# A two-block layer kernel on one core: the first loads and splits in another order, products of x's high parts one tile ahead of its low parts, key products in front of decay and rate products

## The reference

```
mod = silu(c) @ w_ada + b_ada                    # six rows of 1024: shift1, scale1, gate1, shift2, ...
h = rms_norm(x, norm1_w) * (1 + scale1) + shift1
proj = h @ w_in                                  # q, k, v (convolved), z, gates, ...
x = x + gate1 * (mix @ w_o)
h2 = rms_norm(x, norm2_w) * (1 + scale2) + shift2
x = x + gate2 * ((a_path * v_path) @ ffn_w_down) # a_path, v_path from h2 @ ffn_w_up
# second block
p = token_shift(rmsnorm(x, norm1_g_2) @ w_in_2, mu)
r, k, v, wd, ad, gd = split(p)
w = -softplus(-(w0 + tanh(wd) @ w_decay_up)) - 0.5    # decay
a = sigmoid(a0 + ad @ a_up)                           # rate
k = k * (1 + (a - 1) * k_a)
```

## Time and profile before

| what | value |
|---|---|
| median of 3 runs | 2097.0 us (2096.62 to 2098.36) |
| the profiled execution | 2096.3 us, span 2094.5 us |
| TensorE matmul busy | 2009.4 us, 96% of the span |
| VectorE, ScalarE, GpSimd busy | 898.6, 817.8, 989.5 us |
| DMA | 199.59 MB, mean 95 GB/s |
| chain that ended last | TensorE 87%, VectorE 5%, ScalarE 2%, issue 2%, DMA 2%, GpSimd 1% |

### The profile page before, as it was taken

The page is one execution under the profiler, slowest core; times in us unless marked ns, Lnnn a source line. Parts: engine busy times, 40 slices in busy tenths (PEclk is TensorE's granted clock), DMA queues, the critical chain, the costliest instruction groups (busy, mean ns, idle before and its releaser), DMA issues.

```text
span 2094.5 us, 26186 instructions
## 1 busy us (share of the span) xinstructions
PE 2009.4 (96%) x10110; PEld 1630.2 (78%) x10110; DVE 898.6 (43%) x1492; ACT 817.8 (39%) x1092; POOL 989.5 (47%) x767
## 2 busy tenths in 40 slices
PE   6999999999999999999999898999999999999997
PEld 3786896877778887888888577977987788888886
DVE  1678454777432224222200576347974531211101
ACT  3567224336563234232222553334326643222221
POOL 3647614655204564655655372004453265565662
PEclk9999999999999999999999897999999999999999
DMA  6311105631112322222223221003421222222222
GB/s 280 101 61 61 41 1 220 267 105 61 41 41 101 140 87 80 97 101 101 101 101 126 85 69 53 1 31 115 123 90 61 101 101 99 85 98 101 101 101 80
DMA packets 30827, 199.59 MB, mean 95 GB/s; under 512 B 5488, under 2 KB 7664, under 8 KB 9712
## 3 DMA queue, kind: packets, MB, share of 16 engines
q1 hardware_dynamic: 30704, 197.92, 26.2%
HBM read 188.99 MB, written 4.19 MB: 92 GB/s over the span
## 4 chain that ended last, share of the span: by engine, by line
PE 87%; DVE 5%; ACT 2%; issue 2%; DMA 2%; POOL 1%; SPq 0%; ACTq 0%; DVEq 0%; POOLq 0%
PE ps L444 24%; PE ps L445 23%; PE ps L446 23%; PE ps L504 2%; DMA ar<-ada_dram 1%; PE ps L871 1%; PE ps L534 1%; DVE ar L2039 1%; PE ps L858 1%; PE ps L638 1%; PE ps L966 1%; PE ps L926 1%; DMA raw<-panels_dram 1%; PE ps L1176 1%; POOL WL L2570 0%
## 5 line engine op out<-in xcount | busy, mean ns | idle before, releaser
L2570 POOL TENSOR_TENSOR WL<-raw,WH 128x512 fp32r<-128x512 f32 x588 | 780.2, 1327 | 885.6 <-ACT WH L1331 849.2
L444 PE MATMUL ps<-hH,WH 128*128 128x512 f32 x1648 | 660.5, 401 | 20.4 <-DVE xL L1928 6.1
L446 PE MATMUL ps<-hH,WL 128*128 128x512 f32 x1648 | 647.6, 393 | 0.0
L445 PE MATMUL ps<-arR,WH 128*128 128x512 f32 x1392 | 542.2, 390 | 0.0
L1331 ACT CAST WH<-raw 128x2048 fp32r<-128x2048 f32 x147 | 280.9, 1911 | 518.0 <-DMA raw<-panels_dram 516.9
L444 PEld LDWEIGHTS ps<-hH,WH 128*128 128x128 f32 x1648 | 313.5, 190 | 101.2 <-issue 33.9
L446 PEld LDWEIGHTS ps<-hH,WL 128*128 128x128 f32 x1648 | 313.1, 190 | 67.0
L445 PE MATMUL ps<-xL,WH 128*128 128x512 f32 x848 | 336.2, 396 | 0.0
L445 PEld LDWEIGHTS ps<-arR,WH 128*128 128x128 f32 x1392 | 261.7, 188 | 54.4 <-issue 0.2
L444 PE MATMUL ps<-arR,WH 128*128 128x512 f32 x592 | 230.6, 390 | 0.0
L446 PE MATMUL ps<-arR,WL 128*128 128x512 f32 x592 | 230.3, 389 | 0.0
(11 more groups left out here) (391 smaller groups left out, 2259.5 us busy)
## 6 DMA issues: line engine op xcount, KB each, us to landing
raw<-panels_dram SPq DMA_DIRECT2D x145, 1024.0 KB, 4.8
ar<-ada_dram SPq DMA_DIRECT2D x12, 2048.0 KB, 11.9
xT<-xT_dram SPq DMA_DIRECT2D x2, 2048.0 KB, 8.6
out_dram<-xT SPq DMA_DIRECT2D x8, 512.0 KB, 2.6
ar<-ar SPq DMA_DIRECT2D x12, 256.0 KB, 6.8
xT<-out_dram SPq DMA_DIRECT2D x1, 2048.0 KB, 9.2
wide<-wide_dram SPq DMA_DIRECT2D x1, 1024.0 KB, 6.9
ar<-ar SPq DMA_DIRECT2D x8, 128.0 KB, 4.0
```

Source lines behind the costliest of these rows:

```text
L444: mm(out, lhs[0], rhs[0], start=first, stop=False)
L445: mm(out, lhs[0], rhs[1], start=False, stop=False)
L446: return mm(out, lhs[1], rhs[0], start=False, stop=final)
L2570: ins = tt(WL[:, n % SLOTS, c], raw[:, n % SLOTS, c], WH[:, n % SLOTS, c].bitcast(F32), ALU.subtract)
```

## The change

1. SyncE issues block 2 between panel 0 and panel 1 instead of behind both.
2. `panel_due` is -1 for panel 0 and 0 for panel 1, so the two are split apart. ScalarE casts panel 0 ahead of `rstd` and panel 1 behind the copy of rows 2. GpSimd splits panel 0 and then waits for the fourth low part before panel 1.
3. TensorE does the column sums ahead of columns 0; rows 1 and columns 1, rows 3 and columns 3 stand together, behind the first halves of projections 0 and 1 and ahead of those of 2 and 3.
4. In `project_by_k` and `first_projections` the two products with the high part of tile k stand ahead of the product with the low part of tile k - 1, with a wait for each part of its own.
5. In the second block `rkv` 5 stands ahead of `wup` and `rkv` 6 ahead of `aup`; VectorE's `mix(2)` stands ahead of the scans.

The diff, without context lines (line numbers of before, then of the changed kernel):

```diff
@@ -238 +238 @@
-            return 0 if n < 2 else panel_part[0] if n == 2 else panel_part[n - SLOTS + 1]
+            return n - 1 if n < 2 else panel_part[0] if n == 2 else panel_part[n - SLOTS + 1]
@@ -459,0 +460,5 @@
+            def high_products(out, w, x, first):
+
+                mm(out, w[0], x[0], start=first, stop=False)
+                mm(out, w[1], x[0], start=False, stop=False)
+
@@ -464,0 +470,6 @@
+
+                def weights(j, k):
+
+                    c = slice((jobs[j][1] % per) * P, (jobs[j][1] % per + 1) * P)
+                    return [x[:, k, c] for x in ws[j]]
+
@@ -466,4 +477,9 @@
-                for k in range(kt):
-                    pe.wait_ge(*ready(k))
-                    for j, (stage, i) in enumerate(jobs):
-                        last_of[j] = product(pst(stage, i), [x[:, k, (i % per) * P:(i % per + 1) * P] for x in ws[j]], src(k), k == 0, k == kt - 1)
+                for k in range(kt + 1):
+                    if k < kt:
+                        pe.wait_ge(*ready("high", k))
+                        for j, (stage, i) in enumerate(jobs):
+                            high_products(pst(stage, i), weights(j, k), src(k), k == 0)
+                    if k:
+                        pe.wait_ge(*ready("low", k - 1))
+                        for j, (stage, i) in enumerate(jobs):
+                            last_of[j] = mm(pst(stage, i), weights(j, k - 1)[0], src(k - 1)[1], start=False, stop=(k == kt))
@@ -544 +560 @@
-                project_by_k([("up" + sfx, 0), ("up" + sfx, 1)], h_ff, lambda k: norm_step("low", norm, k))
+                project_by_k([("up" + sfx, 0), ("up" + sfx, 1)], h_ff, lambda part, k: norm_step(part, norm, k))
@@ -600,4 +616,10 @@
-                    for k in range(lo, hi):
-                        if j == 0:
-                            pe.wait_ge(*norm_step("low", "rms1", k))
-                        ins = product(pst("qkv", i), [x[:, k, (i % 2) * P:(i % 2 + 1) * P] for x in w], h_mix(k), k == 0, k == KD - 1)
+                    out, c = pst("qkv", i), slice((i % 2) * P, (i % 2 + 1) * P)
+                    for k in range(lo, hi + 1):
+                        if k < hi:
+                            if j == 0:
+                                pe.wait_ge(*norm_step("high", "rms1", k))
+                            high_products(out, [x[:, k, c] for x in w], h_mix(k), k == 0)
+                        if k > lo:
+                            if j == 0:
+                                pe.wait_ge(*norm_step("low", "rms1", k - 1))
+                            ins = mm(out, w[0][:, k - 1, c], h_mix(k - 1)[1], start=False, stop=(k == KD))
@@ -610,2 +631,0 @@
-                pe.wait_ge(sem("one_in_32"), 1)
-                ada_columns(0)
@@ -615,0 +636,2 @@
+                pe.wait_ge(sem("one_in_32"), 1)
+                ada_columns(0)
@@ -619 +640,0 @@
-                ada_rows(1)
@@ -620,0 +642 @@
+                ada_rows(1)
@@ -623 +644,0 @@
-                first_projections(2, 0, HALF)
@@ -624,0 +646 @@
+                first_projections(2, 0, HALF)
@@ -886 +908 @@
-                project_by_k([("wo", 0), ("wo", 1)], mixed, lambda k: part_ready("low", "mix", k))
+                project_by_k([("wo", 0), ("wo", 1)], mixed, lambda part, k: part_ready(part, "mix", k))
@@ -900 +922,2 @@
-                project_by_k([("wag", 0), ("rkv", 4)], h_mix, lambda k: norm_step("low", "rms3", k))
+                project_by_k([("wag", 0), ("rkv", 4)], h_mix, lambda part, k: norm_step(part, "rms3", k))
+                project("rkv", h_mix, 1, i0=5)
@@ -906 +929 @@
-                project("rkv", h_mix, 1, i0=5)
+                project("rkv", h_mix, 1, i0=6)
@@ -910 +933 @@
-                project("rkv", h_mix, 2, i0=6)
+                project("rkv", h_mix, 1, i0=7)
@@ -1191 +1214 @@
-                project_by_k([("wout", 0), ("wout", 1)], merged, lambda k: part_ready("low", "merged", k))
+                project_by_k([("wout", 0), ("wout", 1)], merged, lambda part, k: part_ready(part, "merged", k))
@@ -1236,2 +1259 @@
-            for n in range(2):
-                load_panel("qkv", QKV_ORDER[2 * n] // 2, n)
+            load_panel("qkv", QKV_ORDER[0] // 2, 0)
@@ -1238,0 +1261 @@
+            load_panel("qkv", QKV_ORDER[2] // 2, 1)
@@ -1467 +1490 @@
-                split(0)
+                split(-1)
@@ -1470,0 +1494 @@
+                split(0)
@@ -2329,0 +2354 @@
+                mix(2)
@@ -2334 +2358,0 @@
-                mix(2)
@@ -2602,0 +2627,2 @@
+                split(-1)
+                pool.wait_ge(*norm_step("low", "rms1", HALF - 1))
```

More of the change, by code:

```diff
@@ L618, in block_1 @@
                 first_projections(0, 0, HALF)
+                first_projections(1, 0, HALF)
                 ada_rows(1)
-                first_projections(1, 0, HALF)
                 ada_columns(1)
                 ada_rows(3)
+                ada_columns(3)
                 first_projections(2, 0, HALF)
-                ada_columns(3)
                 first_projections(3, 0, HALF)
```

## The result

| what | before | changed |
|---|---|---|
| median (runs) | 2097.7 us (4: 2096.6 to 2102.7) | 2079.4 us (4: 2073.1 to 2082.4) |
| the profiled execution | 2096.3 us, span 2094.5 | 2082.4 us, span 2080.6 |

The ratio is 0.9904, with a 95% interval of 0.9875 to 0.9933. The forecast was 2079.1. The four runs of the changed kernel lie between 2073.1 and 2082.4, so that the forecast meets the median to 0.3 us is luck.

A forecast was written before the change was run, and what follows sets the result against it. TensorE was taken as the bound, its matmuls busy 2009.4 of 2094.5 us. Savings of 5.5 + 1.7 + 2.2 + 7.8 = 17.2 us from 2096.3 gave 2079.1, range 2073 to 2086.5.

The forecast's parts named there:

- Start, 5.5: At the start, new loads, splits and order on TensorE save 5.5 us, between 3.8 and 6.1.
- GpSimd now waits ...: 0.95 gone: At the start, VectorE's first three scaled tiles no longer run beside GpSimd's split of panel 1; 0.95 us saved.
- The rows 2 block ... is no later than now: At the start, modulation block 2, issued ahead of panel 1, arrives no later than before; no gain counted.
- the break at 18.14 is just what is removed: At the start, unbroken TensorE work from 14.50 may raise the clock near 20, saving 2.3 us more.
- Ahead of the feed-forward, 1.7: First product starts once high part 0 is ready, 1.7 us earlier; ends 0 and 2.3.
- Rival (a): In VectorE-paced stretches and projections behind them the low clock stays, costing 41 us: 2127, slower than before; chance 0.02.
- Second block's first norm and key products, 2.2 + 7.8 = 10.0: Second block: earlier first product saves 2.2 us; key products ahead of the decay products remove stop and slow products, 7.8.
- fills idle time: Second block: mix 2 ahead of the scans uses time in which the scans wait 7.1 us for ScalarE's sigmoids.
- Rival (b): At line 926 TensorE stops for VectorE's key chain, keeping 3.6 of the 7.8 us: 2083.4; chance 0.13.
- (c): At the start, panel 1 lands late and holds ScalarE, first product at 36.7: 2086.8 in all; chance 0.04.
- (d): At the feed-forward and in the second block the low clock eats the earlier start: 13.3 us gained, 2083.0; chance 0.10.
- The gains travel to the end: Behind each changed place TensorE is the bound again and releases the next panels, so the whole 17.2 us lasts.

The follow-up runs named there:

- s_no_gpsimd_wait: Changed kernel without GpSimd's wait for the fourth low part, so it splits panel 1 as soon as it is cast; start stretch 72.9 us against 66.7.
- s_old_sums: Changed kernel with the column sums behind columns 0 again; start stretch 67.3 us against 66.7.
- only_byk: Kernel before with the new order of products in `project_by_k` only; median 2093.1 us, ratio 0.9978.
- best: Changed kernel with rows 3 ahead of columns 1 and modulation columns 10 behind key-value projection 7; median 2070.6 us, ratio to before 0.9871.
- k_mix_back: Changed kernel with VectorE's mix 2 behind the four scans again; one time, 2081.8 us.

## Why the prediction was right, and where it was not

- **The time.** 2079.1 forecast, 2079.4 measured. The range and most terms hold, but the closeness is luck: the start was forecast 2.3 too small, the loss of 2.8 in the middle was not forecast, the two about cancel, and the same kernel measured again had 2076.9.
- **Start, 5.5; measured 7.8.** The mechanism was mis-sized at one step and wrong at another. "GpSimd now waits ...: 0.95 gone" was taken from an execution in which only the first of the three scaled tiles lay beside the split; with VectorE's tiles earlier more lie beside it: in s_no_gpsimd_wait four of its first five operations take 1.65 each, and the clock stays low behind them. The wait is worth up to 6.2 in the changed kernel (5.5 without the later first tile). "The rows 2 block ... is no later than now" was costed at nothing; the load order is worth 2.3. The high products first, 1.6, measured 1.3. The step on the clock, "the break at 18.14 is just what is removed", is refuted by s_old_sums: with the break back, the sums took 2.82. The early clock did come in the changed kernel (sums and columns 0 take 3.79 together in place of 7.31), but not from where the prediction took it, and without the other pieces it is worth little: 0.4 at the first product in only_byk. What decides the moment stays open. Twice 0.8 lost was right, and best takes it back.
- **Ahead of the feed-forward, 1.7; measured 2.4.** In five of nine executions with the new order in this place the stretch is 366.0 to 366.9, in the other four 367.9 to 368.0, against 368.4 to 369.2 in the four without it: at the least 0.4. In the changed kernel the first product comes 0.1 us behind its high part, and the clock is 1.00 from 784 to 790, as its window shows:

```profile
784.00:790.00 6.00, 5.71 (x25) 4.61 (x26) 5.72 (x9) 3.33 (x6) 0.00 (x0) 1.00 0.01 3
```

- **Rival (a) and the rule behind it.** Products paced by VectorE, with short gaps, ran at the full rate in that window. They do not always: in the other four of the nine executions the first six microseconds of this stretch stand at 0.51 to 0.53. In s_old_sums, for one:

```profile
784.00:790.00 6.00, 5.80 (x14) 4.58 (x15) 5.72 (x9) 3.32 (x6) 0.00 (x0) 0.50 0.01 3
```

In all nine the next six are at 1.00. So the low level of rival (a) is real, but here it never outlasts the stretch, and the stretch is still 0.4 to 1.2 us shorter than in the four kernels of the old order. Its price of 41 us did not come. By the rule named in the prediction, of the Trainium skill ("TensorE: Matmul & The Clock Gate", section "A second HAM failure mode: psum-queue depth-cycling"), short idle moments between groups of products would have kept the clock moving between its levels here; the window of the changed kernel at 784 us, at 1.00, does not agree. In s_no_gpsimd_wait the gaps are longer, up to 1.3 us in its list of waits, and there the clock did stay low.
- **Second block's first norm and key products, 2.2 + 7.8 = 10.0; measured 10.4.** Alone, the new order of products gives 2.7 and the keys 9.0, so they overlap by 1.3. The stop is gone and the decay products take 3.70, as forecast. Right in the sum, but that mix 2 "fills idle time" is not why its move matters: k_mix_back shows that it hands a bank back in time.
- **Rival (b).** VectorE's last key operation ends at 1211.23, and TensorE comes at 1213.71: the cover shrank from 3.6 to 2.5 and held. The rival's sum, 17.2 less 4.2, gives 2083.3 and not 2083.4.
- **Rivals (c) and (d).** Panel 1 was cast 24.73 to 26.63 and held nothing back. (d) is in part what the four executions with the low clock at the feed-forward show: 0.4 to 1.2 us left of the 1.7 there.
- **"The gains travel to the end".** True behind 1230, within what executions differ by: the rest is 863.2 before, and 861.5 and 866.9 in two executions of the changed kernel. False in the middle, where "TensorE is the bound" does not hold at columns 10: TensorE came there early, stopped 5.8 us instead of 1.3, and met the low clock behind it. The stop there is 1.3 to 1.5 in the four kernels with the old start or only its GpSimd wait, and 3.4 to 6.8 in seven of the eight with the new start and the old place of columns 10 (middle 695.7 to 697.1 in them); the eighth, k_mix_back, has 1.7 and 692.7. "Waits of some us at places that are free now" was one of the prediction's own signs of being wrong, and this is one. The place before, TensorE and VectorE:

```profile
431.88 1.31 PE L590 MATMUL ps<-cm,ar 128*128 128x1 f32 x8 [1.32 <-DVE ar L2039]
422.30 9.52 DVE L2039 SCALAR_TENSOR_TENSOR ar<-ar,st 128x512 f32<-128x512 f32 x7
```

and VectorE's in k_mix_back:

```profile
414.25 8.61 DVE L2063 SCALAR_TENSOR_TENSOR ar<-ar,st 128x512 f32<-128x512 f32 x7
```

Coming early is only one part. These seven operations take 11.28 us in the changed kernel and in the four other executions that stop 5.7 to 6.8 us; there GpSimd works beside them without pause. They take 9.5 to 9.6 in the two that stop 3.4 and 3.5, and 8.61 in k_mix_back, where GpSimd is idle for 2.79 us beside them. So of the 4.5 us by which the stop grew, 1.8 is VectorE beside GpSimd again, as at the start, and 2.7 is TensorE being further ahead of VectorE. Why GpSimd pauses there in some executions and not in others was not tried.

## What to carry to other kernels

Before costing a start or a norm on the waiting engine, look at which operations of VectorE lie beside GpSimd's: at this start, holding GpSimd back until VectorE's chain is through was worth more than any reordering of TensorE. Follow a gain downstream to the next place where another engine is busy without pause, and put work that waits for nothing in front of that wait. A moved read of a PSUM bank is a price or a gain in itself: ask who gets the bank next, not only who needs the value.

## What the runs showed of the hardware that was not expected

The same kernel's clock falls at different places in different executions. Windows of the changed kernel's first and second profile:

```profile
1366.00:1371.00 5.00, 4.97 (x32) 4.49 (x32) 0.69 (x1) 0.58 (x1) 0.00 (x0) 0.55 0.00 0
1371.00:1376.00 5.00, 4.17 (x9) 1.77 (x6) 0.69 (x1) 3.12 (x3) 1.79 (x2) 0.50 0.32 105
1376.00:1381.00 5.00, 5.00 (x12) 2.09 (x12) 2.07 (x3) 3.21 (x5) 3.29 (x3) 0.92 0.00 0
```

```profile
1366.00:1371.00 5.00, 4.17 (x35) 3.00 (x34) 0.48 (x2) 2.70 (x3) 0.00 (x0) 1.00 0.25 75
1371.00:1376.00 5.00, 5.00 (x13) 2.22 (x12) 2.56 (x4) 4.09 (x6) 4.26 (x4) 1.00 0.08 30
1376.00:1381.00 5.00, 5.00 (x22) 3.88 (x21) 1.25 (x2) 4.76 (x9) 0.82 (x1) 1.00 0.00 0
```

0.50 in the one, 1.00 in the other, a few microseconds apart in the same work. The two spans differ by 5.5 us (2080.6 and 2075.1), and 5.4 of it lie in the last column of the table, where this place is: up to 1366 us the two are 0.4 apart, and at the small products behind it (line 507, at 1408.74 and 1403.86) 4.9. The changed kernel's runs spread over 9 us. What tips the clock was not tried. So a stretch of one profile tells a term of a few microseconds only where several executions show it. An operation of VectorE that takes 0.75 us took up to 1.65 beside a subtraction on GpSimd, while GpSimd's four pieces took 6.46 against 5.32 to 5.37: VectorE paid more than GpSimd. The seven operations at columns 10 agree: 11.28 us beside GpSimd without pause, 5.47 for seven of the same line at 341 us, where GpSimd is idle.
